# Layer-1 key products between the input products of a recurrent layer

## The chip, the cores and the metric

The kernel runs on one core of one Trainium2 chip. The time is device microseconds of one launch; a run of the kernel before took 2101.24 us, the median of three (2099.94 to 2104.44).

## The reference

One inference step of a two-layer decoder: 256 prompt tokens and 8 sequences of 4 sample tokens, 288 tokens of width 1024, all in fp32. Layer 0 is a gated linear recurrence (RG-LRU), layer 1 a state-space block (SSD) with an expert layer behind it. Each layer also attends to 256 memory tokens by keys and values that are projected here and returned. The part that matters:

```
m_l = rms_norm(mem, g_l)                       # l = 0, 1: the same memory, two gains
K_l = m_l @ w_k[l];  V_l = m_l @ w_v[l]        # outputs, used by attention of layer l
proj = rms_norm(x, g) @ w_in                   # 1024 -> 2048: gate branch | xb
xc = causal_conv(xb)                           # 4 taps, carried state in front
r  = sigmoid(blockdiag(w_a) xc + b_a);  i = sigmoid(blockdiag(w_x) xc + b_x)
a  = exp(-8 r softplus(-lam));  u = sqrt(1 - a^2) * (i * xc)
h_t = a_t h_(t-1) + u_t                        # the recurrence
x += (h * gelu(gate)) @ w_out
```

K_1 depends on the memory alone, so it may be computed at any place ahead of layer 1.

## The kernel before

Tokens lie along the free dimension, 128 features to a tile, 8 tiles (KD = 8) to the model width. Every weight matrix is streamed from DRAM in chunks of 128 x 1024 fp32 (512 KB), in the order of the list PLAN (function plan, line 93), which stream_inputs (line 2218) repeats for the data. SyncE issues the loads into a ring of seven places, raw; a load waits until DVE has used what was in its place seven chunks earlier (line 611). A chunk is split for fp32-like precision: ACT copies it to fp32r, the high half w_hi (line 652), DVE subtracts that from the chunk to get the low half w_lo (line 1028), and TensorE takes three matmuls a tile: high by high, low by high, high by low (helper mm3, lines 1590 to 1592). w_hi and w_lo have seven places each.

PLAN also fixes the order of all groups of matmuls, which engine frees the PSUM bank of each (eight banks, in turn: a group takes the bank that the group eight before it had), and how far the conversions run ahead. When ACT or DVE comes to group g, it first converts all chunks up to AHEAD[g], six past the chunk of g (hi_upto, line 644; lo_upto, line 1022), and then waits for the group. The queue of each engine is written out by hand.

The stretch around the change, in the order of TensorE (lines 1660 to 1675): eight gate-branch products, eight input products xb (each one chunk, 24 matmuls of 288 columns, result 128 x 288), then key products 0 and 1 of layer 1 (each one chunk, 24 matmuls of 256 columns), then eight r and eight i products (block diagonal, 3 matmuls each, one chunk for all eight r and one for all i), then key products 2 to 7, the value products of layer 1 (eight chunks, 192 matmuls of 512 columns), then "lru out".

DVE per tile j (line 1159): convert the next chunk and scale xb j+1 into conv (L1152, L1153), wait for ACT's first tap, three more taps (L1100, L1103, L1105) giving xc j, and the low half of the tile before, xc_lo (conv_lo, L1050). ACT per tile (line 743): convert the next high half, wait for DVE's conv j+1, first tap (L738), wait for xc j, its high half xc_hi (L747). Then DVE does the two early key tiles (key_tile, line 1120: convert a chunk, wait for the product, multiply by the memory norm into kmem, L1122), multiplies xc by the i gates (L1171), and does the recurrence: with key tiles 2 to 7 between, it combines a^2 - 1 from POOL's square and ACT's tanh (L1180), multiplies by the root (L1184), scans (L1185), steps the sample sequences (L1194, L1195), and multiplies by the gelu (L1205). ACT has the gates rg and ig (L751, L754), decay and tanh (L762, L765), the root (L769), the write of K_1 (L771), vmem (L689) and the write of V_1 (L692), for which it waits (line 777) before the next stage.

Of the kernel before, what the change touches and what calls it, by code (L numbers as in the profile page):

```python
# [32 lines left out]
F32 = mybir.dt.float32  # L33
# [8 lines left out]
KD = D // P  # L42
# [14 lines left out]
NMEM = 256  # L57
# [29 lines left out]
NSMALL = _at  # L87


EARLY = 2  # L90


def plan():

    def memory(l):
        q = [(("k", l, j), "dve", 1) for j in range(KD)]
        for nb in range(2):
            q += [(("v", l, nb, 0), "act", 3), (("v", l, nb, 1), "act", 1)]  # L100
        return q

    def second(q, key):

        return q[:1] + [(key, "act", 0)] + q[1:]

    p = second(memory(0), "mem norm")
    p += second([(("gate", j), "dve", 1) for j in range(KD)], ("norm", 0))
    p += [(("xb", j), "dve", 1) for j in range(KD)]
    p += memory(1)[:EARLY]  # L110
    p += [(("r", j), "act", int(j == 0)) for j in range(KD)]
    p += [(("i", j), "act", int(j == 0)) for j in range(KD)]
    p += memory(1)[EARLY:]
    p += [(("lru out", j), "dve", 1) for j in range(KD)]

    def attention(l):
        q = second([(("q", l, j), "dve", 1) for j in range(KD)], ("norm", 3 * l + 1))
        q += [(("scores", l, h), "act", 0) for h in range(MH)]
        for b in range(NB):
            if b == NB // 2:  # L120
                q += [(("probs", l, i), "dve", 0) for i in range(4)]
            q += [(("s scores", l, b), "act" if b == NB - 1 else None, 2)]
        q += [(("o", l, j), "dve", 0) for j in range(KD)]
        q += [(("s probs", l), "act", 0)]
        q += [(("s o", l, b), "act" if b == NB - 1 else None, 2) for b in range(NB)]
        return q + [(("s o turn", l), "dve", 0)] + [(("mem out", l, j), "dve", 1) for j in range(KD)]

    p += attention(0)
    up = []
    for f in range(KF):  # L130
        up += [(("f1", f), "dve", 1), (("f3", f), "dve", 1)]
    p += second(up, ("norm", 2))
    p += [(("f2", j), "dve", -(-KF * (j + 1) // 8) + KF * j // -8) for j in range(KD)]
    p += [(("norm", 3), "act", 0)] + [(("xbc", c), "act", 1) for c in range(3)] + [("dt t", "act", 0), ("dt", "dve", 0)]
    p += [(("xbc", c), "act", 1) for c in range(3, NXBC)] + [(("z", c), "act", 1) for c in range(KI)]
    for t in range(3):
        p += [(("acs", t), "dve", 0), (("last", t), "dve", 0)]
        p += [(("xt", t, i), "dve", 0) for i in range(4)]
        p += [(("bt", t), "act", 0), (("cb", t), "dve", 0)]
        for hb in range(10):  # L140
            if hb < 8:
                p += [(("ab", t, hb), "act", 0)] + [(("state ab", hb), "act", 0)] * (t == 1)
            if hb >= 2:
                p += [(("y", t, hb - 2), "dve", 0)]
        if t < 2:
            p += [(("state", t, g), "act" if t == 0 else "dve", 0) for g in range(GROUPS)]
    p += [("s decay", "act", 0)]
    for b in range(NB):
        p += [(("y off", g, b), "dve" if b == NB - 1 else None, (g + 1) % 2) for g in range(GROUPS)]
        p += [(("s state", b, g), "dve", 0) for g in range(GROUPS)]  # L150
    p += [("y off turn", "dve", 0)]
    p += [(("gn", g), "act", 0) for g in range(GROUPS)]
    p += [(("ssd out", j), "dve", 2) for j in range(KD)]
    p += attention(1)
    p += [(("norm", 5), "act", 0), ("logits t", "act", 0), ("logits", "dve", 0)]
    p += [(("ht", i), "act", 0) for i in range(6)]
    p += [("pos", "dve", 0)]
    p += [(("xtok", i), "act", 0) for i in range(6)]
    return p
# [42 lines left out]
def build_program(nc, t):  # L202
# [20 lines left out]
    with ExitStack() as ctx:  # L223
# [7 lines left out]
        def at(name, shape, dtype, offset):  # L231
            return nc.alloc_sbuf_tensor_at(name, [P] + shape, dtype, offset=offset, align_bytes=4)
# [44 lines left out]
        memsq = at("memsq", [KD, NMEM], F32, S[3])  # L277
        mem_hi = [at(f"mem_hi{l}", [KD, NMEM], F32R, (S[6], S[4])[l]) for l in range(2)]
        mem_lo = [at(f"mem_lo{l}", [KD, NMEM], F32R, (S[7], S[10] + 1024)[l]) for l in range(2)]
        kmem = [at(f"kmem{l}", [KD, NMEM], F32, (S[9], S[1])[l]) for l in range(2)]  # L280
        vmem = [at(f"vmem{l}", [2, D], F32, S[8]) for l in range(2)]

        rmt = at("rmt", [NMEM + 2], F32, dt_off + 1472)
# [357 lines left out]
        def _(act):  # L641
# [101 lines left out]
            for j in range(KD):  # L743
                if j + 1 < KD:
                    first_tap(j + 1)
                act.wait_ge(xc_done, j + 1)
                act.activation(xc_hi[:, j, :], xc[:, j, :], ACT.Copy).then_inc(xch_done, 1)  # L747
            hi_upto(AHEAD[KEY["k", 1, EARLY - 1]])
            for j in range(KD):
                b = ready(("r", j), NT)  # L750
                act.activation(rg[:, j, :], b, ACT.Sigmoid, bias=par("b_a")[:, j:j + 1]).then_inc(act_freed, 1)  # L751
# [2 lines left out]
                act.activation(ig[:, j, :], b, ACT.Sigmoid, bias=par("b_x")[:, j:j + 1]).then_inc(act_freed, 1)  # L754
            act.wait_ge(c8_done, 1)
            act.wait_ge(act_freed, FREED[KEY["r", KD - 1]][1])

            for j in range(KD):
                hi_upto(AHEAD[KEY["k", 1, max(j, EARLY)]])
                for k in (2 * (j % 4), 2 * (j % 4) + 1):  # L760
                    if j < 4:
                        act.activation(decay[:, k, :], rg[:, k, :], ACT.Exp, scale=nc8[:, k:k + 1]) \  # L762
                            .then_inc(a_done, 1)
                        act.wait_ge(xi_done, k + 1)
                        act.activation(tanh[:, k, :], rg[:, k, :], ACT.Tanh, scale=nc8[:, k:k + 1]) \  # L765
                            .then_inc(e2_done, 1)
                    else:
                        act.wait_ge(q_done, k + 1)
                        act.activation(expm[:, k, :], expm[:, k, :], ACT.Sqrt, scale=-1.0).then_inc(root_done, 1)  # L769
            act.wait_ge(dve_freed, FREED[KEY["k", 1, KD - 1]][1])  # L770
            act.dma_start(t["out_k"][1], kmem[1][:, :, :]).then_inc(kv_out, 16)  # L771
            hi_upto(AHEAD[KEY["v", 1, 0, 0]])
            for j in range(KD):
                act.wait_ge(y_done, j + 1)
# [244 lines left out]
        def _(dve):  # L1019
# [100 lines left out]
            def key_tile(l, j):  # L1120
                b = ready(("k", l, j), NMEM)
                dve.tensor_tensor(kmem[l][:, j, :], b, rm[:, 0:NMEM], ALU.mult).then_inc(dve_freed, 1)  # L1122
# [34 lines left out]

            conv_input(0)
            for j in range(KD):
                if j + 1 < KD:  # L1160
                    conv_input(j + 1)
                dve.wait_ge(tap_done, j + 1)
                conv_tile(xc[:, j, :], conv[:, j, :], conv_t[:, j % 2, :], par("lru_cw")[:, 4 * j:4 * j + 4], xc_done)
                if j:
                    conv_lo(j - 1)
            conv_lo(KD - 1)
            for j in range(EARLY):
                key_tile(1, j)
            for j in range(KD):
                act_read(("i", j))  # L1170
                dve.tensor_tensor(xc[:, j, :], xc[:, j, :], ig[:, j, :], ALU.mult).then_inc(xi_done, 1)  # L1171
            dve.wait_ge(xi_done, KD)
            for j in range(KD):
                if j >= EARLY:
                    key_tile(1, j)
                for k in (2 * (j % 4), 2 * (j % 4) + 1):
                    if j < 4:
                        dve.wait_ge(sqr_done, k + 1)
                        dve.wait_ge(e2_done, k + 1)
                        dve.scalar_tensor_tensor(expm[:, k, :], expm[:, k, :], 1.0, tanh[:, k, :],  # L1180
                                                 ALU.add, ALU.mult).then_inc(q_done, 1)
                    else:
                        dve.wait_ge(root_done, k + 1)
                        link(dve.tensor_tensor(xc[:, k, :], xc[:, k, :], expm[:, k, :], ALU.mult))  # L1184
                        dve.tensor_tensor_scan(xc[:, k, 0:SEQ], decay[:, k, 0:SEQ], xc[:, k, 0:SEQ], 0.0,  # L1185
                                               ALU.mult, ALU.add)
# [368 lines left out]
        def _(pe):  # L1555
# [104 lines left out]
            for j in range(KD):  # L1660
                square(("gate", j), h_hi, h_lo, NT, hl_done if j == 0 else None, 2 * KD)
                if j == 0:
                    norm(("norm", 0), 0)
            for j in range(KD):
                square(("xb", j), h_hi, h_lo)
            keys(1, range(EARLY))
            for kind in ("r", "i"):
                k = NEED[KEY[kind, 0]] - 1
                for j in range(KD):
                    pe.wait_ge(xcl_done, j + 1)  # L1670
                    product((kind, j), [(k, j, j)], xc_hi, xc_lo)
            keys(1, range(EARLY, KD))
            values(1)
            for j in range(KD):
                square(("lru out", j), xc_hi, xc_lo, NT, yl_done if j == 0 else None)
# [542 lines left out]
def stream_inputs(np, a):  # L2218
# [25 lines left out]
    def memory(l):  # L2244
        return [columns(a["mem_w_k"][l]), rows(a["mem_w_v"][l])]

    parts = memory(0) + [columns(a["lru_w_in"][0])]
    keys_1, values_1 = memory(1)
    parts += [keys_1[:EARLY]]
    for w in ("lru_w_a", "lru_w_x"):  # L2250
        parts += [np.asarray(a[w][0]).transpose(1, 0, 2).reshape(1, P, CH)]
    parts += [keys_1[EARLY:], values_1, columns(a["lru_w_out"][0])]

    def attention(l):
        return [columns(a["mem_w_q"][l]), keys(a["cache_mem_k"][l]), values(a["cache_mem_v"][l]),
# [67 lines left out]
```

## Time and profile before

| | |
|---|---|
| median of three runs | 2101.24 us |
| profiled execution | 2102.84 us, span 2101.3 us, mean granted TensorE clock 0.944 |
| TensorE / DVE / ACT / POOL busy | 91% / 71% / 60% / 9% |
| stretch of the change | from about 94 us (first xb product) to about 211 us (V_1 written) |

The page's second part gives busy tenths in 40 slices of 52.5 us each. The stretch lies in slices 2 to 4, where TensorE has 9, 6 and 8 tenths. A line of the order of time gives start, duration, engine, line, operation, written and read tiles, count, and in brackets the idle time of the engine before it with what ended it. ACT and DVE instructions overlap by about 0.1 us, so what one costs is the distance to the next start.

### The profile page before, as it was taken

The page shows a single profiled execution, that of the slowest core. Times are in us where ns is not written, and L with a number is a line of the kernel's source. Part 1 is how long each engine was busy: PE and PEld are TensorE (multiplying, and loading weights), DVE is VectorE, ACT ScalarE, POOL GpSimd, SP SyncE. Part 2 cuts the span into 40 slices and gives each one's busy share as a digit, 9 for nine tenths or more (in the row PEclk, how much of TensorE's full clock was granted, in tenths as well). Part 3 has the DMA queues.
Part 4 walks back from the last instruction along what each step waited for, and adds up shares of the span by engine and source line. Part 5 has one row for each costly group of instructions (what it writes and reads, how often), then busy time and mean ns, then how long its engine had stood idle before and what let it go on. Part 6 is the DMA issues. An engine that isn't in the chain of part 4 may idle for free.

```text
span 2101.3 us, 32191 instructions
## 1 busy us (share of the span) xinstructions
PE 1918.8 (91%) x10958; PEld 1630.5 (78%) x10958; DVE 1494.5 (71%) x1808; ACT 1266.8 (60%) x1650; POOL 189.3 (9%) x245
## 2 busy tenths in 40 slices
PE   6968889999899988788859999999999999999994
PEld 6968769999799863388638888888888888888883
DVE  7477446664586556653339889898888988898894
ACT  6555335443475432232238788888878788887873
POOL 2001101000141125302010000000000000000001
PEclk9989899999899987699979999999999999999997
DMA  7535677854445005536629999999999999999994
GB/s 278 188 124 182 243 263 285 322 166 142 136 150 175 8 21 180 201 120 242 249 98 388 376 380 359 381 364 370 382 362 381 366 385 360 369 378 356 395 365 147
DMA packets 151106, 558.75 MB, mean 266 GB/s; under 512 B 16496, under 2 KB 16496, under 8 KB 149568
## 3 DMA queue, kind: packets, MB, share of 16 engines
q1 hardware_dynamic: 139248, 508.58, 65.9%
q0 software_dynamic: 7200, 28.56, 3.6%
q10 hardware_dynamic: 4528, 20.05, 2.4%
q8 instruction: 59, 0.97, 0.2%
q14 instruction: 71, 0.58, 0.1%
HBM read 520.61 MB, written 36.52 MB: 265 GB/s over the span
## 4 chain that ended last, share of the span: by engine, by line
PE 75%; issue 8%; DVE 6%; DMA 5%; ACT 4%; POOL 2%; POOLq 0%; SPq 0%; ACTq 0%; DVEq 0%
PE ps L1590 22%; PE ps L1592 22%; PE ps L1591 22%; DMA out_ssd_s<-s_new 2%; DVE w_lo L1028 2%; ACT w_hi L652 2%; DMA raw<-in_stream 1%; PE ps L1800 1%; POOL s_new L2094 1%; PE ps L1942 1%; POOL rt L1986 1%; PE ps L1689 1%; PE ps L1720 1%; PE ps L1831 1%; PE ps L1736 1%
## 5 line engine op out<-in xcount | busy, mean ns | idle before, releaser
L1491 DVE TENSOR_TENSOR w_lo<-raw,w_hi 128x1024 fp32r<-128x1024 f32 x672 | 787.1, 1221 | 48.6 <-ACT w_hi L958 46.9
L958 ACT ACTIVATE w_hi<-raw 128x1024 fp32r<-128x1024 f32 x672 | 705.5, 1060 | 139.3 <-PE ps L1592 122.9
L1028 DVE TENSOR_TENSOR w_lo<-raw,w_hi 128x1024 fp32r<-128x1024 f32 x228 | 285.5, 1263 | 251.0 <-ACT w_hi L652 250.1
L1590 PE MATMUL ps<-w_hi,xe_hi 128*128 128x512 f32 x896 | 358.5, 400 | 4.7 <-DVE w_lo L1491 4.7
L1592 PE MATMUL ps<-w_hi,xe_lo 128*128 128x512 f32 x896 | 354.8, 396 | 0.0
L1591 PE MATMUL ps<-w_lo,xe_hi 128*128 128x512 f32 x896 | 354.3, 395 | 0.0
L652 ACT ACTIVATE w_hi<-raw 128x1024 fp32r<-128x1024 f32 x228 | 237.3, 1051 | 178.8 <-PE ps L1592 105.3
L1590 PE MATMUL ps<-h_hi,w_hi 128*128 128x288 f32 x928 | 281.3, 303 | 19.5 <-DVE h_lo L1054 15.3
L1591 PE MATMUL ps<-h_lo,w_hi 128*128 128x288 f32 x928 | 277.3, 299 | 0.0
L1592 PE MATMUL ps<-h_hi,w_lo 128*128 128x288 f32 x928 | 276.2, 298 | 0.0
L1590 PEld LDWEIGHTS ps<-w_hi,xe_hi 128*128 128x128 f32 x896 | 169.0, 189 | 43.0 <-DVE w_lo L1491 5.1
L1592 PEld LDWEIGHTS ps<-w_hi,xe_lo 128*128 128x128 f32 x896 | 168.7, 188 | 40.0
L1591 PEld LDWEIGHTS ps<-w_lo,xe_hi 128*128 128x128 f32 x896 | 169.1, 189 | 38.4
L1590 PEld LDWEIGHTS ps<-h_hi,w_hi 128*128 128x128 f32 x928 | 176.9, 191 | 23.5 <-DVE h_lo L1054 17.7
L1590 PE MATMUL ps<-w_hi,gt_hi 128*128 128x512 f32 x448 | 178.3, 398 | 0.0
L1592 PEld LDWEIGHTS ps<-h_hi,w_lo 128*128 128x128 f32 x928 | 178.0, 192 | 0.0
L1591 PEld LDWEIGHTS ps<-h_lo,w_hi 128*128 128x128 f32 x928 | 177.5, 191 | 0.4
L1592 PE MATMUL ps<-w_hi,gt_lo 128*128 128x512 f32 x448 | 177.1, 395 | 0.0
L1591 PE MATMUL ps<-w_lo,gt_hi 128*128 128x512 f32 x448 | 177.0, 395 | 0.0
L1592 PEld LDWEIGHTS ps<-w_hi,gt_lo 128*128 128x128 f32 x448 | 84.3, 188 | 20.0
L1591 PEld LDWEIGHTS ps<-w_lo,gt_hi 128*128 128x128 f32 x448 | 84.3, 188 | 19.4
L1590 PEld LDWEIGHTS ps<-w_hi,gt_hi 128*128 128x128 f32 x448 | 84.3, 188 | 19.3
(378 smaller groups left out, 2683.2 us busy)
## 6 DMA issues: line engine op xcount, KB each, us to landing
raw<-in_experts SPq DMA_DIRECT2D x672, 512.0 KB, 5.5
raw<-in_stream SPq DMA_DIRECT2D x264, 512.0 KB, 4.2
rest<-in_stream SPq DMA_DIRECT2D x28, 512.0 KB, 5.0
x_rows<-zeros ACTq DMA_DIRECT2D x1, 13824.0 KB, 58.6
out_ssd_s<-s_new POOLq DMA_DIRECT2D x16, 512.0 KB, 7.2
xs<-x_rows POOLq DMA_DIRECT2D x9, 512.0 KB, 4.6
y_rows<-ye POOLq DMA_DIRECT2D x9, 512.0 KB, 7.3
out_k<-kmem ACTq DMA_DIRECT2D x2, 1024.0 KB, 6.6
```

The costliest lines, as they stand in the source:

```text
L652: act.activation(w_hi[:, o % HL, :], landing_place(k), ACT.Copy).then_inc(hi_done, 1)
L958: act.activation(w_hi[:, (NSPLIT + p) % HL, :], raw[:, slot, :], ACT.Copy) \
L1028: dve.tensor_tensor(w_lo[:, o % HL, :], landing_place(k), w_hi[:, o % HL, :].bitcast(F32), ALU.subtract).then_inc(lo_done, 1)
L1491: dve.tensor_tensor(w_lo[:, (NSPLIT + p) % HL, :], raw[:, (NRING + p) % RAW, :], w_hi[:, (NSPLIT + p) % HL, :].bitcast(F32), ALU.subtract) \
L1590: pe.matmul(out, l_hi, r_hi, start=start, stop=False)
L1591: pe.matmul(out, l_hi, r_lo, start=False, stop=False)
L1592: return pe.matmul(out, l_lo, r_hi, start=False, stop=stop)
L1689: a = pe.matmul(out[:, tt * NMEM:(tt + 1) * NMEM], q[:, j, tt * P:(tt + 1) * P], kt[:, j, :], start=(dd == 0), stop=(dd == 1))
L1720: a = pe.matmul(out, vt[:, m, j * P:(j + 1) * P], prt[:, m, j // 2, :], start=(m == 0), stop=(m == 1))
L1736: a = pe.matmul(out_o[32 * hd:32 * hd + 32, :], pm[:, m, col:col + 32], values_b[:, hd * NMEM:(hd + 1) * NMEM], start=(b == 0 and m == 0), ...
L1800: a = pe.matmul(out[:, j * n:(j + 1) * n], adt_s[half][0:n, tt, 4 * hb + j:4 * hb + j + 1].broadcast_to([n, n]), tri_r[:, :] if tt < 2 els ...
L1831: a = pe.matmul(o, xt[0:n, hd * 64:(hd + 1) * 64], mt[(tt * 8 + hb) % 4][0:n, j * n:(j + 1) * n], start=True, stop=(tt != 1))
```

## The change

The plan puts key product j of layer 1 between input products j+1 and j+2 (the last two behind input product 7) and all eight of them ahead of the r and i products. TensorE's queue, the stream of chunks, DVE's and ACT's queues follow. DVE does key tile j-1 at the head of tile j of the convolution loop and key tile 7 behind it. ACT writes K_1 to DRAM right behind the convolution, in place of behind the roots. The key tiles lie where the decay will be (S[0]) and no more over the high half of the layer's input (S[1]), which the input products still read; so ACT waits for the write of K_1 (kv_out, 48) before it writes the first decay.

```diff
@@ plan
-    p += [(("xb", j), "dve", 1) for j in range(KD)]
-    p += memory(1)[:EARLY]
+    p += [(("xb", j), "dve", 1) for j in range(2)]
+    for j in range(KD):
+        p += memory(1)[j:j + 1] + [(("xb", j + 2), "dve", 1)] * (j + 2 < KD)
     p += [(("r", j), "act", int(j == 0)) for j in range(KD)]
     p += [(("i", j), "act", int(j == 0)) for j in range(KD)]
-    p += memory(1)[EARLY:]
+    p += memory(1)[KD:]
@@ places
-        kmem = [at(f"kmem{l}", [KD, NMEM], F32, (S[9], S[1])[l]) for l in range(2)]
+        kmem = [at(f"kmem{l}", [KD, NMEM], F32, (S[9], S[0])[l]) for l in range(2)]
@@ ACT
                 if j + 1 < KD:
                     first_tap(j + 1)
+                if j:
+                    hi_upto(AHEAD[KEY["k", 1, j - 1]])
                 act.wait_ge(xc_done, j + 1)
                 act.activation(xc_hi[:, j, :], xc[:, j, :], ACT.Copy).then_inc(xch_done, 1)
-            hi_upto(AHEAD[KEY["k", 1, EARLY - 1]])
+            hi_upto(AHEAD[KEY["k", 1, KD - 1]])
+            act.wait_ge(dve_freed, FREED[KEY["k", 1, KD - 1]][1])
+            act.dma_start(t["out_k"][1], kmem[1][:, :, :]).then_inc(kv_out, 16)
...
             act.wait_ge(act_freed, FREED[KEY["r", KD - 1]][1])
+            act.wait_ge(kv_out, 48)
 
             for j in range(KD):
-                hi_upto(AHEAD[KEY["k", 1, max(j, EARLY)]])
...
-            act.wait_ge(dve_freed, FREED[KEY["k", 1, KD - 1]][1])
-            act.dma_start(t["out_k"][1], kmem[1][:, :, :]).then_inc(kv_out, 16)
@@ DVE
             for j in range(KD):
+                if j:
+                    key_tile(1, j - 1)
                 if j + 1 < KD:
                     conv_input(j + 1)
...
             conv_lo(KD - 1)
-            for j in range(EARLY):
-                key_tile(1, j)
+            key_tile(1, KD - 1)
...
             for j in range(KD):
-                if j >= EARLY:
-                    key_tile(1, j)
@@ TensorE
+            for j in range(2):
+                square(("xb", j), h_hi, h_lo)
             for j in range(KD):
-                square(("xb", j), h_hi, h_lo)
-            keys(1, range(EARLY))
+                keys(1, [j])
+                if j + 2 < KD:
+                    square(("xb", j + 2), h_hi, h_lo)
...
-            keys(1, range(EARLY, KD))
             values(1)
```

## Rows read from the trace of the kernel before

**Rows 1.** The page, part 1: busy time of the engines and share of the span.
```profile
PE 1918.8 (91%) x10958; PEld 1630.5 (78%) x10958; DVE 1494.5 (71%) x1808; ACT 1266.8 (60%) x1650; POOL 189.3 (9%) x245
```

**Rows 2.** Busy time by stretch: TensorE's idle stretch, with TensorE, clock, DMA alone; two later stretches.
```profile
126.90:145.60 18.70, 3.48 (x11) 0.59 0.25 85
...
150.00:152.50 2.50, 2.50 (x18) 2.50 (x18) 1.05 (x1) 2.50 (x7) 0.00 (x0) 0.86 0.67 256
...
195.00:200.00 5.00, 5.00 (x26) 4.25 (x26) 1.52 (x2) 0.71 (x1) 0.00 (x0) 0.99 0.82 288
```

**Rows 3.** Order of time of TensorE: last xb, keys, gates, values.
```profile
116.47 0.30 PE L1590 MATMUL ps<-h_hi,w_hi 128*128 128x288 f32 x1
...
119.67 0.28 PE L1590 MATMUL ps<-mem_hi,w_hi 128*128 128x256 f32 x1
...
125.42 0.30 PE L1590 MATMUL ps<-xc_hi,w_hi 128*128 128x288 f32 x1
...
145.77 0.58 PE L1590 MATMUL ps<-xc_hi,w_hi 128*128 128x288 f32 x1 [3.73 <-DVE kmem L1122]
...
192.03 0.79 PE L1590 MATMUL ps<-w_hi,mem_hi 128*128 128x512 f32 x1 [5.81 <-DVE w_lo L1028]
```

**Rows 4.** The chain of waits, start, us and what, behind the recurrence.
```profile
190.84 1.15 DVE w_lo L1028
...
203.43 7.07 DMA out_v<-vmem
```

**Rows 5.** Order of time of DVE: one tile of the convolution, then the early key tiles.
```profile
122.65 1.23 DVE L1028 TENSOR_TENSOR w_lo<-raw,w_hi 128x1024 fp32r<-128x1024 f32 x1 [1.09 <-ACT w_hi L652]
123.79 0.42 DVE L1152 TENSOR_TENSOR conv<-ps,rs 128x256 f32<-128x256 f32 x1
...
127.48 1.23 DVE L1028 TENSOR_TENSOR w_lo<-raw,w_hi 128x1024 fp32r<-128x1024 f32 x1 [1.09 <-ACT w_hi L652]
...
144.06 1.23 DVE L1028 TENSOR_TENSOR w_lo<-raw,w_hi 128x1024 fp32r<-128x1024 f32 x1 [0.44 <-ACT w_hi L652]
145.21 0.42 DVE L1122 TENSOR_TENSOR kmem<-ps,rm 128x256 f32<-128x256 f32 x1
145.54 1.22 DVE L1028 TENSOR_TENSOR w_lo<-raw,w_hi 128x1024 fp32r<-128x1024 f32 x1
```

**Rows 6.** Order of time of ACT, from the convolution to the write of the keys.
```profile
121.57 1.04 ACT L652 ACTIVATE w_hi<-raw 128x1024 fp32r<-128x1024 f32 x1
...
142.99 2.93 ACT L652 ACTIVATE w_hi<-raw 128x1024 fp32r<-128x1024 f32 x3
...
147.24 3.24 ACT L751 ACTIVATE rg<-ps,small 128x288 f32<-128x288 f32 x8
...
154.32 1.17 ACT L652 ACTIVATE w_hi<-raw 128x1024 fp32r<-128x1024 f32 x1
155.51 1.28 ACT L762 ACT_TABLE_LOAD   x1
156.81 0.54 ACT L762 ACTIVATE decay<-rg,nc 128x288 f32<-128x288 f32 x1
...
161.09 0.52 ACT L762 ACTIVATE decay<-rg,nc 128x288 f32<-128x288 f32 x1
...
179.88 0.34 ACTq L771 DMA_DIRECT2D out_k<-kmem  x1
```

**Rows 7.** Order of time of DVE in the recurrence.
```profile
158.63 3.36 DVE L1180 SCALAR_TENSOR_TENSOR expm<-expm,tanh 128x288 f32<-128x288 f32 x4 [3.00 <-ACT tanh L765]
161.91 1.69 DVE L1028 TENSOR_TENSOR w_lo<-raw,w_hi 128x1024 fp32r<-128x1024 f32 x1
...
168.92 0.45 DVE L1184 TENSOR_TENSOR xc<-xc,expm 128x288 f32<-128x288 f32 x1
...
184.39 0.83 DVE L1205 TENSOR_TENSOR y_lru<-xc,gate 128x288 f32<-128x288 f32 x2
```

**Rows 8.** The page, part 6: DMA issues, size, median us to landing.
```profile
out_k<-kmem ACTq DMA_DIRECT2D x2, 1024.0 KB, 6.6
```

More of the change, by code:

```diff
@@ L87 @@
 NSMALL = _at
-EARLY = 2
 def plan():
@@ L2245, in memory @@
         return [columns(a["mem_w_k"][l]), rows(a["mem_w_v"][l])]
-    parts = memory(0) + [columns(a["lru_w_in"][0])]
+    w_in = columns(a["lru_w_in"][0])
+    parts = memory(0) + [w_in[:KD + 2]]
     keys_1, values_1 = memory(1)
-    parts += [keys_1[:EARLY]]
+    for j in range(KD):
+        parts += [keys_1[j:j + 1], w_in[KD + 2 + j:KD + 3 + j]]
     for w in ("lru_w_a", "lru_w_x"):
         parts += [np.asarray(a[w][0]).transpose(1, 0, 2).reshape(1, P, CH)]
-    parts += [keys_1[EARLY:], values_1, columns(a["lru_w_out"][0])]
+    parts += [values_1, columns(a["lru_w_out"][0])]
     def attention(l):
```

## The prediction

> **What bounds the kernel now.** I began with the shares by engine, then took the chain of waits over 125 to 200 us, then the order of time of each engine there; the change touches nothing outside that stretch. TensorE is busy 91% of the span [rows 1], so work that only changes its place is worth something only where TensorE stands still. In the stretch it does so twice. First, from 126.9 to 145.6 us, it is busy for 3.48 of 18.70 us [rows 2]: the gate products r wait one by one for the convolved tiles, and the seventh, at 145.77, waits 3.73 us for DVE to free key tile 0 [rows 3]. Second, before 192.03 it is idle for 5.81 us, because DVE, which has the recurrence to do, converts the next weight chunk only at 190.84 [rows 3, 4]. From 125 to 190 us the chain of waits lies in DVE and ACT. At its end stands the write of the values, 7.07 us from 203.43, on which ACT waits [rows 4], and everything later hangs on that. So the price of the change is by how much it moves the chunk conversion at 190.84.
>
> The stretch has three parts: (a) the convolution ring, (b) the gates, (c) the recurrence. The change moves six key tiles out of (c), and two from behind (a), into (a). On DVE a key tile costs one chunk conversion (the low half), 123.79 - 122.65 = 1.14 us, and one multiplication, 145.54 - 145.21 = 0.33 us [rows 5]: 1.47 us. On ACT it costs one high half, 2.93 / 3 = 0.98, of which 0.95 us to the next start [rows 6].
>
> **(a) The ring gets longer.** Over one tile of the ring DVE goes from the low half at 122.65 to the one at 127.48, 4.83 us [rows 5]. It isn't busy all that time: the page gives 1.09 us of idle before the low half, with ACT's high half as its releaser. One would like the key tile to go into that idle time. I hold that it does not. ACT's high half at 121.57 [rows 6] follows its conversion of the convolved tile, which waits for DVE's last tap; the low half waits for that high half; conv, taps and the next tile come behind it. It is one closed loop over both engines. In the changed kernel ACT issues two high halves behind the convolved tile (the new hi_upto behind first_tap asks for nothing that first_tap has not taken already), DVE does low half, key tile, low half, convolution input, taps. The first high half is as late as before, the second (0.95 us later) is hidden behind DVE's first low half and key tile (1.47 us), and all of DVE's 1.47 us comes on top: 4.83 + 1.47 = 6.30 us.
>
> TensorE does not take over as the bound: an input product takes 119.67 - 116.47 = 3.20 us, a key product (125.42 - 119.67) / 2 = 2.87 us [rows 3], together 6.07 us, and it starts far ahead: it is through with all eight input products at 119.67, while DVE takes the fifth of them at 123.79 [rows 5]. With 6 x 2.87 us more in between it is through with the last key product at about 125.42 + 17.2 = 142.6 us, before DVE gets there.
>
> Tiles 1 to 6 add 6 x 1.47 = 8.8 us. Tile 7 had neither a chunk nor the wait for ACT, and now gets both with a key tile: 1.09 + 1.47 = 2.6 us. So the low half that stood at 144.06 (key tile 0) [rows 5] stands at 144.06 + 11.4 = 155.5 us, now for key tile 7. **+11.4 us.**
>
> **(b) The gates** wait for more in front. Key tile 7 is freed at 155.5 + 1.14 + 0.41 = about 157.0. ACT waits for that in order to issue the write of the keys (moved here from 179.88, 0.34 us, some 0.44 with its surroundings), and behind it stand one high half (0.95) and the table load (1.28 to 1.30) [rows 6]. So the first gate comes at 157.0 + 0.44 + 0.95 + 1.30 = 159.7, against 147.24 [rows 6], which was 3.2 us behind its low half and is now 4.2: **+1.1 us.** Behind them, from 147.24 to the first decay at 156.81 [rows 6], are 9.57 us: eight r, a high half, eight i, a high half (154.32 to 155.51, 1.19 us), a load. The last high half goes, since chunks are now asked for earlier: **-1.1 us**, decay 0 at 156.8 + 11.4 = 168.2 us. The r and i products run behind these without a say: the last r when key 7 is freed, the eight i from 160.4 on (a bank from the first r gate). One is an eighth of an input product, 0.40 us, and at most 0.80 at the low of TensorE's two clocks (granted: 0.59 on average over its idle stretch [rows 2]); eight take at most 6.4 us, to 166.8, and ACT wants the eighth at 166.5. Tight, worth 0.3 us at most.
>
> **(c) The recurrence gets shorter.** Before, from decay 0 to the first product with the root at 168.92 it was 12.11 us [rows 6, 7]. Now ACT has eight pairs of decay and tanh at (161.09 - 156.81) / 5 = 0.856 us [rows 6] = 6.9, the load 1.3 and a root of 0.4, and DVE with its eight combinations (four in 3.36 us beside POOL's squares, from 1.82 us behind decay 0 [rows 7]) is through at 8.5, no later than ACT: 8.7 us. **-3.4 us.** From 168.92 to 184.39 [rows 7] DVE needed 15.47 us: eight scans with their products, small steps, and the last three key tiles. These go, 3 x 1.47: **-4.4 us.**
>
> The sum is +11.4 + 1.1 - 1.1 - 3.4 - 4.4 = +3.6 us; with the gaps between instructions followed one by one I get 3.77, and take **+3.7 us**: the outputs of the recurrence begin at 188.1, the chunk that TensorE waits for is converted from 194.5, and the products restart at 195.7. What hides and what doesn't: the 17.2 us of key products that TensorE no longer has behind the gates are worth nothing, because value products still stop at the same chunk (DVE's low halves reach just as far ahead of the recurrence as before). They only make the second idle of TensorE longer: value products from about 164.7, 16.5 us as before (169.7, where the key products end, to 192.03 - 5.81) and up to 2 for the clock, until 183, and then 13 us idle where there were 5.8. All that follows 190.84, the write of 7.07 us included, is the same work in the same order.
>
> Costs without a row of their own. **The clock behind the longer idle:** behind 145.77 the mean of 0.86 over 150.0 to 152.5 says that the full clock was back at 150.7, 4.9 us later; behind 192.03 the 0.99 over 195 to 200 says 195.1, 3.1 us later [rows 2, 3]. If the longer idle makes it the first, 1.8 us more run at half speed: 0 to 0.9 us. I take 0, the row at the same place. **POOL's copies of the last convolution inputs,** now beside the key tiles' low halves: such a low half beside POOL took 1.69 instead of 1.23 us [rows 5, 7], so 0 to 0.6 for the one or two that meet; I take 0, since POOL's copies are small. **The moved write** (1 MB of keys at 157 instead of 179.88) lands before the value write is issued in both kernels: 0, and its wait is a rival below. **kmem's new place** costs nothing but that wait. The i products: 0 to 0.3. So the bounds are 3.0 to 5.5 us.
>
> The profiled execution has a span of 2101.3 us and a time of 2102.84, so by this sum 2106.5; that execution is 1.6 above the median of 2101.24. The shift does not depend on it, so 2101.24 + 3.7 = **2104.9 us.** About 0.2%, 4.2 us, is what a measurement of this kernel can tell from no change, and my sum ends just below it.
>
> **Rivals.**
> *The ring has room (faster).* If ACT's high half for the key tile were done before the convolved tile is, DVE would not wait, and the tile would take its own work only: 4.83 - 1.09 + 1.47 = 5.21 us. Seven tiles times 1.09 is 7.6 us less: 3.7 - 7.6 = -3.9, 2097.3 us. For it: the 1.09 us of idle are there in each tile and DVE is the engine that everything waits for. Against: the order on ACT's queue, by which both high halves stand behind the convolved tile. It decides once a high half starts before DVE's last tap.
>
> *The moved write of the keys holds ACT (slower).* kmem now lies where the decay is written, so ACT waits for the write before decay 0. It is issued at 157.1 and wanted at 167.0, 9.9 us later; such a write took 6.6 us [rows 8] and the value write 7.07 [rows 4]. Beside seven chunk loads and more it might take 12: 2.1 us on top, +5.8, 2107.0. It decides from 9.9 us on, and everything behind, POOL's squares and DVE, waits.
> The Trainium skill, in Perfetto Trace Analysis, section "DMA Instruction — HWDGE (DVE, Sync)", says that the semaphore of a transfer follows the confirmed write, which "can cause a surprisingly long delay especially when the write target is HBM". It has no figure; by it this rival would be likelier than I make it, while the two writes of this trace stay 3 us below the point.
>
> *Nothing comes of it (within 0.2%).* Small gains in (b) and (c), such as gates that find their products ready, make up for the ring: 0, 2101.2 us.
>
> **Chances.** The forecast mechanism, the ring and its refund, has 0.70, of which I put 0.40 below 4.2 us and 0.30 above it (bounds 3.0 to 5.5, and a median that moves by a microsecond or two). The faster rival 0.12, the slower one 0.10, nothing 0.08. So faster 0.12, within 0.2% 0.48, slower 0.40. The range leaves out the faster rival and the far end of the slower one: 2099.8 to 2108.0 us.
>
> **What would show it.** Right: low halves in pairs on DVE with 6.3 us from pair to pair, and an idle of 1.1 us only before the first of a pair; TensorE without a gap until about 142.6; decay 0 near 168.2; outputs of the recurrence from 188, the restart of TensorE near 195.7 behind an idle of some 13 us. Wrong: pairs 5.2 us apart (the first rival); ACT idle before the first decay with the key write as releaser (the second); or a restart that lies more than 2 us from 195.7. Where the restart is right and the time isn't, the stages behind it would have moved, which I have excluded.

## The result, and the profile after

| | before | changed |
|---|---|---|
| median of 19 runs each | 2102.83 us | 2106.82 us |
| lowest to highest | 2099.29 to 2104.98 | 2104.70 to 2109.69 |
| profiled execution | 2102.84, span 2101.3 | 2106.14, span 2104.5 |

The ratio is 1.0021, 95% interval 1.0014 to 1.0028: the change costs 4.4 us (2.9 to 5.9), where 3.7 was forecast. The changed kernel is slower: the interval leaves out no change, though the loss is only about 0.2% of the time.

**First the two traces have to be laid over each other.** The fences hold two rows of each kernel, before first: one from the chain of waits (start, us, what) and the low half of DVE's first tile in the ring, in order of time.

```profile
22.82 1.22 PE ps L1637 x2
...
112.97 1.23 DVE L1028 TENSOR_TENSOR w_lo<-raw,w_hi 128x1024 fp32r<-128x1024 f32 x1 [1.46 <-ACT w_hi L652]
```

```profile
22.78 0.70 PE ps L1637 x2
...
111.38 1.23 DVE L1029 TENSOR_TENSOR w_lo<-raw,w_hi 128x1024 fp32r<-128x1024 f32 x1 [1.46 <-ACT w_hi L651]
```

At the ring the changed kernel's record is 1.59 us ahead, and the offset has two halves. The first products of the launch, 70 us ahead of the change, took 1.22 us in one record and 0.70 in the other (granted clock 0.50 and 0.87 from 22.8 to 24.1 us), and when the values of layer 0 are issued to DRAM the offset is 0.80 (72.41 and 71.61 us). DVE waits for that write before it scales the first gate product (line 1140), and it took 9.0 us to landing in one record and 8.2 in the other: 0.79 more. The edit has no part in either, so 1.59 is added to all distances below between starts in the two records; distances within one record need nothing. So aligned, layer 1's attention loads its keys 4.4 us later (954.0 and 956.8 us), and the spans, 3.2 us apart as they stand, differ by 4.8.

DVE of the changed kernel in order of time (start, duration, engine, line, operation, tiles, count, idle before it with its releaser):

```profile
117.68 1.22 DVE L1029 TENSOR_TENSOR w_lo<-raw,w_hi 128x1024 fp32r<-128x1024 f32 x1 [1.09 <-ACT w_hi L651]
118.82 0.42 DVE L1123 TENSOR_TENSOR kmem<-ps,rm 128x256 f32<-128x256 f32 x1
119.15 1.22 DVE L1029 TENSOR_TENSOR w_lo<-raw,w_hi 128x1024 fp32r<-128x1024 f32 x1
120.28 0.42 DVE L1153 TENSOR_TENSOR conv<-ps,rs 128x256 f32<-128x256 f32 x1
...
123.98 1.23 DVE L1029 TENSOR_TENSOR w_lo<-raw,w_hi 128x1024 fp32r<-128x1024 f32 x1 [1.09 <-ACT w_hi L651]
...
153.95 1.23 DVE L1029 TENSOR_TENSOR w_lo<-raw,w_hi 128x1024 fp32r<-128x1024 f32 x1 [0.49 <-ACT w_hi L651]
155.09 0.42 DVE L1123 TENSOR_TENSOR kmem<-ps,rm 128x256 f32<-128x256 f32 x1
...
175.71 0.46 DVE L1184 TENSOR_TENSOR xc<-xc,expm 128x288 f32<-128x288 f32 x1 [0.65 <-ACT expm L772]
...
186.77 0.83 DVE L1205 TENSOR_TENSOR y_lru<-xc,gate 128x288 f32<-128x288 f32 x2
```

These answer to [rows 5] and [rows 7]. From pair to pair it is 123.98 - 117.68 = 6.30 us where one low half took 4.83. The old idle time of 1.09 us still stands, before the first of the pair, and the second follows without any: the key tile did not go into the idle time, it went behind it.

ACT over the same stretch, answering to [rows 6]:

```profile
155.54 0.34 ACTq L751 DMA_DIRECT2D out_k<-kmem  x1
155.98 1.06 ACT L651 ACTIVATE w_hi<-raw 128x1024 fp32r<-128x1024 f32 x1 [2.06 <-DVE kmem L1123]
157.06 1.28 ACT L754 ACT_TABLE_LOAD   x1
158.35 3.25 ACT L754 ACTIVATE rg<-ps,small 128x288 f32<-128x288 f32 x8
...
165.69 1.28 ACT L765 ACT_TABLE_LOAD   x1
166.99 0.54 ACT L765 ACTIVATE decay<-rg,nc 128x288 f32<-128x288 f32 x1
```

TensorE and the write of the values, answering to [rows 3] and [rows 4]; then busy time by stretch (stretch, us, busy us and count of TensorE, weight load, DVE, ACT, POOL, then clock, DMA share, GB/s), which answers to [rows 2]:

```profile
141.70 0.28 PE L1592 MATMUL ps<-mem_hi,w_lo 128*128 128x256 f32 x1
...
194.40 0.79 PE L1590 MATMUL ps<-w_hi,mem_hi 128*128 128x512 f32 x1 [13.56 <-DVE w_lo L1029]
...
206.00 0.34 ACTq L691 DMA_DIRECT2D out_v<-vmem  x1
...
213.22 1.06 ACT L651 ACTIVATE w_hi<-raw 128x1024 fp32r<-128x1024 f32 x1 [7.25 <-DMA out_v<-vmem]
```

```profile
120.00:142.00 22.00, 22.00 (x178) 22.00 (x177) 18.23 (x38) 10.17 (x15) 0.00 (x0) 1.00 0.56 179
142.00:160.00 18.00, 6.49 (x28) 5.07 (x28) 12.00 (x21) 9.22 (x14) 3.29 (x16) 0.63 0.51 163
...
180.00:195.30 15.30, 1.74 (x6) 1.18 (x5) 14.61 (x35) 6.91 (x13) 2.29 (x4) 0.64 0.03 10
```

TensorE looks better up to 142 us: not a gap at the full clock, where it was idle from 126.9 before. It comes back behind: from 142 to 160 us TensorE is idle for 18.00 - 6.49 = 11.51 us, and before 194.40 for 13.56, where there were 5.81. The page's shares hardly show the change; TensorE is at 91% as in [rows 1]:

```profile
PE 1921.8 (91%) x10958; PEld 1630.5 (77%) x10958; DVE 1495.2 (71%) x1808; ACT 1266.4 (60%) x1650; POOL 189.0 (9%) x245
```

### The profile page after: what moved, and what is told of

It is laid out like the page before. It is cut to its first block, busy times and chain, and to the rows that moved or that the text cites. A ratio compares the mean times of both kernels' runs of the same rounds, so it can differ in the third digit from the quotient of the medians.

```text
span 2104.5 us, 32191 instructions
## 1 busy us (share of the span) xinstructions
PE 1921.8 (91%) x10958; PEld 1630.5 (77%) x10958; DVE 1495.2 (71%) x1808; ACT 1266.4 (60%) x1650; POOL 189.0 (9%) x245
## 4 chain that ended last, share of the span: by engine, by line
PE 72%; issue 8%; DVE 8%; DMA 5%; ACT 5%; POOL 2%; POOLq 0%; ACTq 0%; SPq 0%; DVEq 0%
PE ps L1590 21%; PE ps L1592 21%; PE ps L1591 21%; DVE w_lo L1029 2%; ACT w_hi L651 2%; DMA out_ssd_s<-s_new 2%; DMA raw<-in_stream 1%; PE ps L1802 1%; POOL s_new L2096 1%; PE ps L1944 1%; DMA out_v<-vmem 1%; POOL rt L1988 1%; PE ps L1691 1%; PE ps L1722 1%; PE ps L1833 1%
```

## The experiments

Each was timed in five rounds against the kernel before on the same chip. Theory A is the forecast: the ring is a closed loop over ACT and DVE. Its rivals are the prediction's. Ratios are to the kernel before; in the same terms the changed kernel has 1.0021 (1.0014 to 1.0028). A record of an experiment is aligned as above, at the last instruction ahead of the edit. A difference in us is (ratio - 1) times the 2103 us of the kernel before, and between two variants the difference of two such.

**1. The high half ahead of the wait.** In the changed kernel ACT converts the high half of its next two chunks before it waits for the convolved tile. The edit moves one request and no work.

```diff
                 if j + 1 < KD:
                     first_tap(j + 1)
-                if j:
-                    hi_upto(AHEAD[KEY["k", 1, j - 1]])
+                hi_upto(AHEAD[KEY["xb", j + 2] if j + 2 < KD else KEY["k", 1, j]])
                 act.wait_ge(xc_done, j + 1)
```

> The changed kernel, with one edit on ACT's queue: in tile j of the convolution loop the high halves that DVE wants at the head of tile j+1 are asked for before ACT waits for the convolved tile, not behind it. Closed-loop theory (the key tile costs its whole 1.47 us because ACT's high half stands behind DVE's last tap): the idle before the first low half of a pair goes (1.46 + 5 x 1.09 + 1.07 us, perhaps 0.5 more), pairs stand 5.2 us apart instead of 6.3, and the kernel is 8 us faster than the changed one, about 4 us faster than the kernel before (2098.5 beside 2102.8). Rival (TensorE's products, 6.07 us a pair, or the work outside the ring set the pace): pairs stay near 6.1 to 6.3 us apart and the time stays within 2 us of the changed kernel, 4 us above the kernel before.

Measured: 2098.87 against 2102.40 us, ratio 0.9981 (0.9971 to 0.9990). DVE in order of time:

```profile
115.41 1.22 DVE L1028 TENSOR_TENSOR w_lo<-raw,w_hi 128x1024 fp32r<-128x1024 f32 x1
116.55 0.42 DVE L1122 TENSOR_TENSOR kmem<-ps,rm 128x256 f32<-128x256 f32 x1
...
120.54 1.22 DVE L1028 TENSOR_TENSOR w_lo<-raw,w_hi 128x1024 fp32r<-128x1024 f32 x1
```

The idle time is gone and the pairs are 5.13 us apart, 1.17 less than 6.30. TensorE restarts 9.2 us earlier than in the changed kernel (185.66 us in a record that stands 0.41 later). So it was the order on ACT's queue that kept the 1.09 us there: this is the prediction's faster rival made true, and its price, -3.9 us on the kernel before, is what the chip gave (-4.0).

**2. The same request in the kernel before.** No key product is moved.

```diff
                     first_tap(j + 1)
+                if j + 2 < KD:
+                    hi_upto(AHEAD[KEY["xb", j + 2]])
                 act.wait_ge(xc_done, j + 1)
```

> The kernel before, with the same edit as the first: the high half for the next tile of the convolution is asked for before the wait for the convolved tile. Closed-loop theory: tiles of DVE stand 3.74 us apart instead of 4.83, idle of 1.46 + 5 x 1.09 = 6.9 us goes, and the kernel is 6.9 us faster than before (2095.9 beside 2102.8), which is also faster than the changed kernel with that edit, by some 3 us. Rival (the ring is not what ends last; TensorE's products at 3.20 us a tile and its later idle do): a gain under 2 us.

Measured: 2095.89 against 2102.40 us, ratio 0.9969 (0.9960 to 0.9978), -6.5 us. DVE's tiles in order of time:

```profile
115.03 1.22 DVE L1030 TENSOR_TENSOR w_lo<-raw,w_hi 128x1024 fp32r<-128x1024 f32 x1
...
118.69 1.22 DVE L1030 TENSOR_TENSOR w_lo<-raw,w_hi 128x1024 fp32r<-128x1024 f32 x1
```

A tile takes 3.66 us in place of 4.83. The stall that the change lengthened was there before it and can be taken away without it; with the loop open, moving the keys into the ring (experiment 1) is 2.5 us worse than leaving them (this one): -4.0 against -6.5. The two intervals just touch, but both kernels were timed in the same rounds, and there their medians are 3.0 us apart.

**3. The key write without its wait.** The decay goes to S[1], as before the change; nothing that it overwrites is being written out.

```diff
-        decay = at("decay", [KD, NT], F32, S[0])
+        decay = at("decay", [KD, NT], F32, S[1])
...
-            act.wait_ge(kv_out, 48)
```

> The changed kernel with the decay in another place (S[1], free by then) and so without ACT's wait for the write of the keys. Theory: that wait costs nothing, since the write is issued 11.5 us before the first decay; the time is that of the changed kernel, +4 us on the kernel before, within 1 us. Rival (the moved write holds ACT): 1 us or more of the 4 us go.

Measured: 2107.45 us, ratio 1.0027 (1.0016 to 1.0037); no difference from the changed kernel. ACT in order of time:

```profile
155.39 0.34 ACTq L751 DMA_DIRECT2D out_k<-kmem  x1
...
166.84 0.54 ACT L764 ACTIVATE decay<-rg,nc 128x288 f32<-128x288 f32 x1
```

From issue to decay 0 it is 11.45 us with the wait and without it, and the write landed 6.7 us after its issue in both. The slower rival's wait is free.

**4. The key write behind the i gates,** on top of experiment 3.

```diff
-            act.wait_ge(dve_freed, FREED[KEY["k", 1, KD - 1]][1])
-            act.dma_start(t["out_k"][1], kmem[1][:, :, :]).then_inc(kv_out, 16)
... behind the i gates:
+            act.wait_ge(dve_freed, FREED[KEY["k", 1, KD - 1]][1])
+            act.dma_start(t["out_k"][1], kmem[1][:, :, :]).then_inc(kv_out, 16)
```

> As the kernel without the wait, and the issue of the key write, with its wait for key tile 7, stands behind the i gates instead of ahead of the r gates. Theory (the gates start late because ACT stands behind key tile 7, the term of +1.1 us and some idle before it): the gates start 2.1 us earlier, at 1 us behind the last high half plus the table load; 0.4 us comes back for the issue ahead of the decay: 1.7 us faster than the changed kernel, +2.3 on the kernel before. Rival (the gate products of TensorE, at the low clock and behind key tile 7's bank, set this place): nothing, +4 us.

Measured: 2104.87 us, ratio 1.0016 (1.0008 to 1.0025). ACT in order of time:

```profile
154.78 1.99 ACT L651 ACTIVATE w_hi<-raw 128x1024 fp32r<-128x1024 f32 x2
156.78 1.28 ACT L752 ACT_TABLE_LOAD   x1
158.08 3.24 ACT L752 ACTIVATE rg<-ps,small 128x288 f32<-128x288 f32 x8
...
163.33 0.34 ACTq L757 DMA_DIRECT2D out_k<-kmem  x1
```

Before the gates ACT no longer waits 2.06 us for DVE's last key tile. This record stands 1.91 us later than the changed kernel's, so the gates are 2.2 us earlier. The stage behind starts 1.9 us earlier (213.19 against 213.22, with the 1.91). By time, -1.1 us, it can't be told from the changed kernel; the gates are the firmer reading.

**5. Four key tiles in the ring, four in the recurrence,** in the layout of experiment 3, with the keys written behind the roots as before.

```diff
+RINGED = 4
-        p += memory(1)[j:j + 1] + [(("xb", j + 2), "dve", 1)] * (j + 2 < KD)
+        p += memory(1)[j:j + 1] * (j < RINGED) + [(("xb", j + 2), "dve", 1)] * (j + 2 < KD)
...
-                if j:
+                if 1 <= j <= RINGED:
                     key_tile(1, j - 1)
```

> Half of the change: key tiles 0 to 3 in the convolution loop, none right behind it, 4 to 7 in the recurrence as before (decay in S[1], the keys written behind the roots as before). Theory (price by tile, with its own refund): four tiles of the ring at 6.30 instead of 4.83 us, +5.9; ACT has one high half ahead of the gates instead of three, -1.9; one key tile instead of three between the first decay and the first product with the root, 9.4 us instead of 12.1, -2.7; the last three as before. +1.3 us on the kernel before (2103.7 beside 2102.4). Rival (the loss comes from the gates behind a full ring or from TensorE's longer idle, not from each tile): 0 or less, or the whole +4.

Measured: 2104.67 against 2103.46 us, ratio 1.0008 (0.9999 to 1.0016). DVE in order of time:

```profile
130.80 1.23 DVE L1029 TENSOR_TENSOR w_lo<-raw,w_hi 128x1024 fp32r<-128x1024 f32 x1 [1.09 <-ACT w_hi L654]
...
137.09 1.22 DVE L1029 TENSOR_TENSOR w_lo<-raw,w_hi 128x1024 fp32r<-128x1024 f32 x1 [1.09 <-ACT w_hi L654]
141.92 1.23 DVE L1029 TENSOR_TENSOR w_lo<-raw,w_hi 128x1024 fp32r<-128x1024 f32 x1 [1.09 <-ACT w_hi L654]
```

One kernel shows both tiles: 6.29 us with a key tile, 4.83 without. The outputs of the recurrence begin 1.30 us later than before, after alignment, as expected. The time alone, +1.7 us with an interval from -0.2 to +3.4, can't be told from the kernel before, and its interval still touches that of the whole change.

**6. The idle time filled.** Experiment 2, four early key tiles in place of two, and the high halves run further ahead; one more key tile goes where DVE waits for the first tanh (the 3.00 us of [rows 7]).

```diff
-EARLY = 2
+EARLY = 4
...
+                hi_upto(AHEAD[KEY["xb", j + 2] if j + 2 < KD else KEY["k", 1, j + 2 - KD]] + min(j // 2, 3))
                 act.wait_ge(xc_done, j + 1)
...
             dve.wait_ge(xi_done, KD)
+            key_tile(1, EARLY)
             for j in range(KD):
-                if j >= EARLY:
+                if j > EARLY:
                     key_tile(1, j)
```

> The kernel before with the early high half, and key tiles where DVE stands idle: 0 to 3 right behind the ring (their products fill TensorE's idle stretch, their high halves are made ahead in the ring), 4 between the i products and the first combination, 5 to 7 in the recurrence as before. Theory (DVE's own work on the chain sets the time; its idle of 3.2 and 3.0 us in the gates is free): the gates end no later than with two key tiles behind the ring, three key tiles go from between decay and root, -3.4 us on top of the -6.5 of the early high half: -10 us (2092.4 beside 2102.4). Rival (the r products wait for four key tiles' banks, or TensorE starts the value products too late): -6.5 or worse.

Measured: 2091.09 against 2103.46 us, ratio 0.9952 (0.9939 to 0.9964), -10.1. DVE in order of time:

```profile
149.16 1.23 DVE L1029 TENSOR_TENSOR w_lo<-raw,w_hi 128x1024 fp32r<-128x1024 f32 x1 [0.23 <-ACT w_hi L652]
150.47 0.42 DVE L1123 TENSOR_TENSOR kmem<-ps,rm 128x256 f32<-128x256 f32 x1
...
174.58 0.83 DVE L1207 TENSOR_TENSOR y_lru<-xc,gate 128x288 f32<-128x288 f32 x2
```

The first two rows are that key tile, and it does go into idle time: the first combination on DVE starts at 152.12, 3.2 us behind the i products' end at 148.94, where it was 3.0 without the tile. Here a key tile was free where DVE waits for the work that ACT and POOL have of their own, and not free in the ring, where ACT waits for DVE.

**7. The value write's wait taken away,** on top of experiment 1; POOL, which reads the values back later, has its own wait for them.

```diff
-            act.wait_ge(kv_out, 64)
             residual(("lru out",), gains("g_mem", 0))
```

> The changed kernel with the early high half, and without ACT's wait for the write of the values ahead of the residual (the key tiles no longer lie under the layer's next high half, so nothing that the residual writes is being read). Theory: the residual's ring of eight tiles starts 7.1 us earlier, and all of it reaches the end: -4 - 7 = -11 us on the kernel before (2091.4). Rival (POOL's load of keys and values, which still waits for the write, ends last in the attention, or TensorE's products do): -4 to -6.

Measured: 2092.57 against 2103.46 us, ratio 0.9954 (0.9941 to 0.9968), -9.7, where experiment 1 with the wait has -4.0: 5.7 us for the wait. ACT, then DVE, in order of time:

```profile
198.03 0.34 ACTq L691 DMA_DIRECT2D out_v<-vmem  x1
198.47 1.06 ACT L651 ACTIVATE w_hi<-raw 128x1024 fp32r<-128x1024 f32 x1 [0.47 <-ACT vmem L688]
```

```profile
206.52 2.38 DVE L1027 TENSOR_TENSOR w_lo<-raw,w_hi 128x1024 fp32r<-128x1024 f32 x1 [1.46 <-ACT w_hi L651]
```

So the write did stand on the path, and 5.7 of the 6.91 us that ACT waited for it in experiment 1 are gained, as far as two ratios with intervals of 2 to 3 us can tell. One low half that now runs beside POOL's first work of the next stage takes 2.38 us in place of 1.23, which gives back about 1.1.

**8. Both (6 and 7),** with the wait on the earlier writes (48) kept ahead of the values.

```diff
+            act.wait_ge(kv_out, 48)
             values(1)
-            act.wait_ge(kv_out, 64)
```

> The kernel with the filled idle times, and without the wait for the value write (ACT waits instead for the key write before it issues the value write, when that is long done). Theory: the two gains add, -10 - 7 = -17 us on the kernel before (2085.4). Rival as in the run before: -10 to -12.

Measured: 2087.16 against 2103.46 us, ratio 0.9928 (0.9915 to 0.9941), -15.1 (-17.9 to -12.4), two short of the expectation, which the interval still holds. Low halves of the next stage lie beside POOL here too, but I made no run on those two microseconds.

**9. DVE's low halves further ahead,** on top of 8: behind the scans DVE converts the chunks that TensorE will want and does the sample steps after them.

```diff
+            lo_upto(AHEAD[KEY["v", 1, 0, 0]] - 1)
+
             def tok(buf, k):
```

> The fastest kernel so far (idle times filled, no wait for the value write), and DVE converts the last two value chunks behind the scans, ahead of the recurrence's outputs, not behind them. Theory: 2.3 us more on DVE's chain, but TensorE does the last 24 value products (8.2 us with the low clock) beside it and starts the output product when the outputs are there: 4.7 us less than without, 20 us below the kernel before (2083). Rival (the second idle of TensorE costs nothing, the ring of the residual sets its own start): +2.3 us on the kernel without.

Measured: 2083.79 against 2102.96 us, ratio 0.9902 (0.9887 to 0.9918), -20.6. It is the fastest of all kernels here. DVE of experiment 9 in order of time, then of experiment 8:

```profile
171.80 2.34 DVE L1029 TENSOR_TENSOR w_lo<-raw,w_hi 128x1024 fp32r<-128x1024 f32 x2
...
192.22 0.45 DVE L1067 TENSOR_TENSOR x_res<-x_res,ps 128x288 f32<-128x288 f32 x1
```

```profile
198.03 0.45 DVE L1067 TENSOR_TENSOR x_res<-x_res,ps 128x288 f32<-128x288 f32 x1
```

The residual comes 5.8 us earlier, in a record that stands 1.1 earlier: 4.7 us, for two conversions at another place. TensorE's idle time of 6.8 us before the last value products (experiment 8) is gone, with the same work on DVE in another order; 3.66 us of idle before the output products are left.

**10. The same line in the changed kernel,** whose idle time there is 13.56 us.

> The changed kernel with only that edit: the last two value chunks converted on DVE behind the scans. Theory (the key products taken out from behind the gates are worth nothing in the changed kernel since TensorE stands 13.6 us before those chunks): the value products end before the outputs of the recurrence do, the value write goes out 5.5 us earlier, and so the kernel is 5.5 us faster than the changed one, 1.5 us below the kernel before. Rival (that idle is harmless): 2.3 us slower than the changed kernel, +6.3.

Measured: 2104.91 against 2102.96 us, ratio 1.0012 (1.0003 to 1.0021): 1.9 us better than the changed kernel, where 5.5 was expected, and the two intervals overlap. The expectation failed. ACT in order of time, and the busy time of a stretch (columns as above):

```profile
202.84 0.34 ACTq L691 DMA_DIRECT2D out_v<-vmem  x1
...
212.71 1.06 ACT L651 ACTIVATE w_hi<-raw 128x1024 fp32r<-128x1024 f32 x1 [9.90 <-DMA out_v<-vmem]
```

```profile
205.00:210.00 5.00, 5.00 (x40) 5.00 (x39) 0.00 (x0) 0.00 (x0) 0.00 (x0) 1.00 0.93 376
```

The write is issued 3.9 us earlier (206.00 - 202.84 = 3.16, and this record stands 0.77 later), not 5.5. The output products do start 4.9 us earlier (197.50 against 201.60), but behind a new idle time of 3.46 us, and the granted clock was 0.50 from 197.5 to 200.8 us: from their first product to the issue it is 5.34 us in place of 4.40. Then ACT waits 9.90 us for the write instead of 7.25, so of 3.9 us 2.65 go back.

Why this write is longer is not shown. The DMA share of 0.93 above does not set it apart: over the changed kernel's own wait of 7.25 us the share is 0.93 too, at 334 GB/s. By the packets of the two traces the write's first packet started 3.7 us behind the issue where it was 2.0, its packets were spread over 5.7 us where it was 4.75, and 1.87 MB of chunk loads ran beside it where there were 1.38. That fits loads that are ahead of it on the same DMA engines, but no run takes them away. The Trainium skill, in Perfetto Trace Analysis, section "DMA Instruction — HWDGE (DVE, Sync)", says that the semaphore of a transfer follows the confirmed write. In both traces ACT went on 0.4 us behind the write's last packet, so what made the wait longer lies before that.

## Why the prediction was right

By its own steps, with forecast and measured side by side (us; starts against the kernel before with the 1.59):

| step | forecast | measured |
|---|---|---|
| one tile of the ring | 6.30 | 6.30 |
| (a) last low half of the ring | +11.4 | 153.95 - 144.06 + 1.59 = +11.48 |
| (b) low half to first gate | +1.1 | 4.40 - 3.18 = +1.22 |
| (b) first gate to decay 0 | -1.1 | 8.64 - 9.57 = -0.93 |
| (c) decay 0 to first root product | -3.4 | 8.72 - 12.11 = -3.39 |
| (c) root product to outputs | -4.4 | 11.06 - 15.47 = -4.41 |
| outputs of the recurrence | +3.7 | 186.77 - 184.39 + 1.59 = +3.97 |
| restart of TensorE | 195.7 | 194.40 + 1.59 = 195.99 |
| time | +3.7 | +4.0 by medians, +4.4 by the ratio |

**(a)** is shown: the pair distance by the trace, its cause by experiment 1, where the idle time goes once ACT's request stands ahead of its wait, and the price per key tile again by experiment 5. **(b), (c)** came out to 0.2 us each, with both parts of (b) off the same way, +0.12 and +0.17. **The last key product** ended at 142.0, 143.6 after alignment, where 142.6 was the forecast; the stretch to 142 has no gap and the ring went on for 12 us more, so TensorE was never the bound.

**Costs without a row.** The clock behind the longer idle: 0 was taken. The first 24 value products took 7.20 us where they had 7.00, so 0.2 of the 0 to 0.9. That this pair of records shows so little is in part luck: in the records of experiments 1 to 8 the same 24 products took 7.03 to 8.24 us, in no order with the idle time ahead of them (7.91 behind 4.97, 8.24 behind 8.93, 7.03 behind 13.67 us), so one record of each kernel can't size this term. POOL's copies: 0, as taken. The i products: eight i gates without a wait, 0. The write of the values took 7.25 instead of 7.12 us, 0.1 more. Together +0.3 us, and with the steps' own +0.27 the stage behind starts 213.22 - 210.51 + 1.59 = 4.3 us later, close to the measured 4.4.

**The rivals.** *The ring has room* was wrong for this code and right in its condition and in its price (experiment 1). *The moved write holds ACT* fell with experiment 3: from the issue to the table load of the decay it was 165.69 - 155.54 = 10.15 us (9.9 was the forecast), and ACT had no idle time there; the write had landed after 6.7. The margin was smaller than the prediction says, though. It has the writes of the trace stay 3 us below the point of 9.9 us, but the same trace holds a third write of 1 MB, that of layer 0's values at 72.41 us, which took 9.0 us to landing, 0.9 below the point, and 8.2 in the changed kernel's record. The chance of 0.10 should have been weighed with that row. The value write I had taken as 7.07 us of constant length: right for this change (7.25 against 7.12 us of waiting), and wrong in experiment 10, where it was 9.90. *Nothing comes of it* asked for refunds that aren't there.

**What stayed rough.** The forecast of 2104.9 stands 1.9 under the median of 2106.82, and 1.6 of that is the kernel before, whose median went from 2101.24 in three runs to 2102.83 in nineteen. I put 0.48 on a loss under 0.2% and 0.40 on one above; it came out on the line.

## What to carry to other kernels

Idle time before an instruction is room for more work only if its releaser is not itself waiting for that engine: follow the releaser back over its own queue until you either come to real work or come home. If you come home, don't fill the gap, open the loop; here one request moved ahead of a wait was worth 6.5 us, more than the whole reordering was about. And here a busier TensorE ahead of a wait that did not move brought nothing: ask what the next stage hangs on (here a write of 1 MB), and count only what moves that.

## What the runs showed that I had not expected

- A write of 1 MB to DRAM took 6.89 (experiment 5) to 7.25 us until ACT went on, and 9.90 us in experiment 10; that of layer 0's values took 9.0 us to landing in the record before and 8.2 in the changed one. The mean DMA share beside these five was 0.90 to 0.97 where I looked (0.91 beside 7.12, 0.93 beside 7.25, 0.90 beside 9.0, 0.97 beside 8.2), so the share doesn't tell them apart. Issuing it 3.9 us earlier brought 1.3 by the trace of experiment 10.
- DVE's low half of 128 x 1024 took 1.23 us alone and 2.38 us beside POOL in experiment 7 (POOL issues a load and adds squares from 206.4 to 207.8 us), more than the 1.69 of [rows 7].
- Two launches of nearly the same program differ by 1.6 us before any edited line: 0.8 by the issue of layer 0's values, with TensorE's first products at another granted clock, and 0.8 by the length of that write. A comparison of starts without alignment would have put the loss at 2.4 us.
- The time of the first 24 products behind the second idle time does not follow its length: 7.00 us behind 5.81, 7.20 behind 13.56, 8.24 behind 8.93 (experiment 5), 7.03 behind 13.67 (experiment 7).
